# Feed-forward products with the activations standing and 512 weight columns moving

## The reference, cut to what matters

```
x = x + g1 * y                                   # y: the mixer's output
h = rmsnorm(x) * (1 + sc2) + sh2                 # 256 tokens x 1024
x = x + g2 * ((silu(h @ W_gate) * (h @ W_up)) @ W_down)     # width 2816
```

## Time and profile before

| | |
|---|---|
| time, 3 executions | 1597.55, 1596.38, 1596.40 us |
| median | 1596.4 us |
| the profiled execution | span 1595.4 us from its first to its last instruction, 1.0 us under the median |
| PE busy | 1539.4 us, 96% of the span, 12451 matmul records |
| DVE, ACT, POOL busy | 1198.9 us (75%), 785.7 us (49%), 110.9 us (7%) |
| memory traffic | 383.77 MB, 241 GB/s on average |

### The profile page before, as it was taken

One profiled execution on the slowest core, in us unless ns is written; L12 is line 12 of the kernel. 1 busy time (PEld: TensorE's weight loads), 2 busy tenths in 40 slices (PEclk: granted clock), 3 DMA queues, 4 the chain that ended last, 5 costly groups with the idle time before them and its releaser, 6 DMA issues.

```text
span 1595.4 us, 30716 instructions
## 1 busy us (share of the span) xinstructions
PE 1539.4 (96%) x12451; PEld 1470.4 (92%) x12460; DVE 1198.9 (75%) x1724; ACT 785.7 (49%) x1033; POOL 110.9 (7%) x111
## 2 busy tenths in 40 slices
PE   2889999999999999999999999999999999999998
PEld 1868999999999999999899999789999988899998
DVE  6898877778578777865587777968777788676665
ACT  2455433356464333565543335565333577655543
POOL 0150000000000000011000000220000063200000
PEclk9999999999999999999999999999999999999999
DMA  9855987856258878573478785446878655345550
GB/s 389 356 187 213 372 312 298 308 188 236 80 211 327 324 297 325 207 258 132 159 318 323 306 318 206 148 159 253 348 300 312 235 174 183 120 162 183 182 184 26
DMA packets 54907, 383.77 MB, mean 241 GB/s; under 512 B 6420, under 2 KB 6932, under 8 KB 9264
## 3 DMA queue, kind: packets, MB, share of 16 engines
q1 hardware_dynamic: 50976, 363.75, 60.5%
q0 software_dynamic: 3856, 18.97, 3.3%
HBM read 381.62 MB, written 4.22 MB: 242 GB/s over the span
## 4 chain that ended last, share of the span: by engine, by line
PE 85%; DVE 8%; DMA 3%; ACT 1%; issue 1%; POOL 1%; SPq 0%; DVEq 0%; ACTq 0%
PE PS L1929 74%; PE PS L1950 3%; DVE wlo L1359 2%; DVE adar L1384 1%; DMA CST<-cst_in 1%; PE PS L2076 1%; PE PS L2126 1%; DMA adar<-ada 1%; DVE SCR L1546 1%; PE PS L2103 1%; PE PS L2004 1%; ACT whi L930 1%; DMA raw<-ada 1%; PE PS L1976 1%; PE PS L1963 1%
## 5 line engine op out<-in xcount | busy, mean ns | idle before, releaser
L1929 PE MATMUL PS<-hhi,whi 128*128 128x256 f32 x2496 | 714.7, 286 | 2.7 <-DVE wlo L1359 2.6
L1929 PE MATMUL PS<-hlo,whi 128*128 128x256 f32 x2496 | 708.3, 284 | 0.0
L1929 PE MATMUL PS<-hhi,wlo 128*128 128x256 f32 x2496 | 708.1, 284 | 0.0
L1359 DVE TENSOR_TENSOR wlo<-raw,whi 128x2048 fp32r<-128x2048 f32 x229 | 526.3, 2300 | 238.4 <-ACT whi L930 238.1
L930 ACT ACTIVATE whi<-raw 128x2048 fp32r<-128x2048 f32 x234 | 447.0, 1912 | 479.4 <-PE PS L1929 467.1
L1929 PEld LDWEIGHTS PS<-hhi,whi 128*128 128x128 f32 x2496 | 480.9, 193 | 9.8 <-issue 7.7
L1929 PEld LDWEIGHTS PS<-hlo,whi 128*128 128x128 f32 x2496 | 481.3, 193 | 1.3 <-issue 1.2
L1929 PEld LDWEIGHTS PS<-hhi,wlo 128*128 128x128 f32 x2496 | 481.1, 193 | 0.0
L1384 DVE CUSTOM_DVE_ANT_0 adar<-adar,CB 128x1024 f32<-128x1024 f32 x232 | 277.0, 1233 | 9.7 <-DMA adar<-ada 9.7
L1929 PE MATMUL PS<-ahi,whi 128*128 128x256 f32 x968 | 274.5, 284 | 1.1 <-DVE alo L1879 1.1
L1929 PE MATMUL PS<-alo,whi 128*128 128x256 f32 x968 | 273.9, 283 | 0.0
(11 more groups left out here) (240 smaller groups left out, 1319.7 us busy)
## 6 DMA issues: line engine op xcount, KB each, us to landing
raw<-weights SPq DMA_DIRECT2D x234, 1024.0 KB, 6.4
adar<-ada SPq DMA_DIRECT2D x104, 1024.0 KB, 5.8
adar<-ada POOLq DMA_DIRECT2D x12, 1024.0 KB, 5.4
raw<-ada SPq DMA_DIRECT2D x4, 1024.0 KB, 15.2
bias_rows<-bias_of_distance POOLq DMA_DIRECT2D x1, 3072.0 KB, 13.7
adar<-bias_rows POOLq DMA_DIRECT2D x8, 256.0 KB, 3.2
CST<-cst_in SPq DMA_DIRECT2D x1, 1128.0 KB, 22.7
CB<-c_in SPq DMA_DIRECT2D x2, 512.0 KB, 3.8
```

The costliest lines, as they stand in the source:

```text
L1359: v.tensor_tensor(wlo[:, u % CV, :], raw[:, u % RAW, :], whi[:, u % CV, :].bitcast(F32), ALU.subtract).then_inc(lo_done, 1)
L1929: m = pe.matmul(o, w(a), h(b), start=first and k_ == 0, stop=last and k_ == 2, skip_group_check=True)
```

## The change

In the four layers that are not `b2`, a feed-forward step's gate and up columns are packed side by side, 512 columns, and its two units hold the first and the second half of the 1024 input channels (`row_units`). In `row_half` a 128 x 128 block of the activations (128 channels, 128 tokens) stands and 512 weight columns move; the result has tokens on the partitions, one bank for each half of the tokens (`row_banks`). A unit is then 24 matmuls of 512 columns. Silu and the product are done on that layout. `turn_act` brings the product back to channels on partitions with four PE transposes, and `ffn_hi` and `act_lo` read the turned bank in PSUM. `first_rows` takes the place of `project_pair` for step 0.

In all five layers `down` has the activations standing and 512 columns of the down weights moving, for the first ten steps; the sums have tokens on the partitions (`down_rows`). ACT then copies the four banks to SBUF (`down_copies`), PE turns them into the eight half banks with 16 transposes (`turn`), and the eleventh step is added as before (`down_last`). The last two steps are written out behind a loop of four instead of five. The conditions on which engines wait change with the layout, and `act_lo` moves in DVE's queue from behind the third `lo` of a step to behind the first `ada_sum` of the next.

The layout in PSUM:

```diff
+        def row_banks(s_):
+            return PS[:, 2 * (s_ % 2):2 * (s_ % 2) + 2, :]
+        def turned_bank(s_):
+            return bank[2 * (s_ % 2)]
+        def down_rows(t, h):
+            return bank[4 + 2 * h + t]
+        def down_copy(t, h):
+            return SCR[:, (0, 1, 4, 5)[2 * h + t], :]
         def down_bank(c):
-            return bank[4 + c // 2][:, S * (c % 2):S * (c % 2) + S] if c < C - 1 else bank[2][:, 0:S]
+            return bank[(2, 2, 3, 3, 4, 4, 5, 6)[c]][:, S * (c % 2):S * (c % 2) + S]
```

ACT:

```diff
-                        act.wait_ge(pe_unit, (f if s_ == 0 else f + 2 + 3 * (s_ - 1)) + 1 + 6 * add)
+                        act.wait_ge(pe_unit, (f if s_ == 0 else f + 2 + 3 * (s_ - 1)) + 2 + 6 * add)
-                    act.activation(SCR[:, 2, :], src, ACT.Silu).then_inc(sg_done, 1)
+                        act.activation(two(SCR[:, 2, :]), row_banks(s_)[:, :, 0:S], ACT.Silu).then_inc(sg_done, 1)
+                        act.wait_ge(a_turned, STEPS * l + s_ + 1 + 2 * add)
+                        src = turned_bank(s_)[:]
+                    act.activation(ahi[:, s_ % 2, :], src, ACT.Copy).then_inc(ahi_done, 1)
+                def down_copies(h):
+                    for t in range(2):
+                        if (h, t) == (1, 1):
+                            act.wait_ge(pe_unit, f + FFN_UNITS - 1)
+                        else:
+                            act.wait_ge(y_part, 3 * l + 2 * h + t + 1)
+                        act.activation(down_copy(t, h), down_rows(t, h)[:], ACT.Copy).then_inc(y_copied, 1)
...
                         hi(f + 4 + 3 * st, add=i)
+                        if kind != "b2":
+                            ffn_hi(st, add=i)
                         hi(f + 5 + 3 * st, add=i)
                         ffn_gate(1 + st, add=i)
                         hi(f + 6 + 3 * st, add=i)
-                        ffn_hi(1 + st, add=i)
+                        if kind == "b2":
+                            ffn_hi(1 + st, add=i)
+                down_copies(0)
+                if kind != "b2":
+                    ffn_hi(STEPS - 1)
+                down_copies(1)
```

DVE:

```diff
                 ffn_act(0)
                 lo(f + 3)
-                act_lo(0)
+                if kind == "b2":
+                    act_lo(0)
                 if more:
                     ada_sum(a0, 1, a0 % 2)
                 with v.Fori(0, 5) as i:
...
                         lo(f + 4 + 3 * st, add=i)
                         if more:
                             ada_sum(a0 + 1 + st + 2 * i, 0, (a0 + 1 + st) % 2)
+                        if kind != "b2":
+                            act_lo(st, add=i)
                         lo(f + 5 + 3 * st, add=i)
                         if more:
                             ada_sum(a0 + 1 + st + 2 * i, 1, (a0 + 1 + st) % 2)
                         ffn_act(1 + st, add=i)
                         lo(f + 6 + 3 * st, add=i)
-                        act_lo(1 + st, add=i)
+                        if kind == "b2":
+                            act_lo(1 + st, add=i)
```

PE:

```diff
+                def rows_of(u, s_, c, t, parts, first=False):
+                    for x, a in parts:
+                        m = pe.matmul(row_banks(s_)[:, t, :], hs[x][:, c, P * t:P * t + P], ws[a][:, u % CV, 512 * (c % 4):512 * (c % 4) + 512],
+                                      start=first and (x, a) == (0, 0), stop=c == C - 1, skip_group_check=True)
+                    return m
+                def row_half(u, s_, h, add):
+                    unit_ready(u, add)
+                    for t in range(2):
+                        for c in range(4 * h, 4 * h + 4):
+                            m = rows_of(u, s_, c, t, ((0, 0), (0, 1), (1, 0)), c == 0)
+                    m.then_inc(pe_unit, 1)
+                def first_rows(u, m):
+                    warm(4, (4, 5, 6, 7))
+                    unit_ready(u)
...
+                    for c in range(1, C):
+                        pe.wait_ge(norm_lo, C * m + c + 1)
+                        if c == 4:
+                            unit_ready(u + 1)
+                        for t in range(2):
+                            e = rows_of(u + c // 4, 0, c, t, ((0, 0), (0, 1), (1, 0)))
+                        if c % 4 == 3:
+                            e.then_inc(pe_unit, 1)
+                def turn_act(s_, add=0):
+                    pe.wait_ge(a32_done, STEPS * l + s_ + 1 + 2 * add)
+                    for j in range(2):
+                        for t in range(2):
+                            e = pe.transpose(turned_bank(s_)[:, S * j + P * t:S * j + P * t + P], SCR[:, 3, S * t + P * j:S * t + P * j + P], ident)
+                    e.then_inc(a_turned, 1)
...
-                    for c in range(C):
-                        o = down_bank(c)
-                        for t in range(2):
-                            m = split_product(o, lambda a: ws[a][:, u % CV, D * t + P * c:D * t + P * c + P],
-                                              lambda x: acts[x][:, s_ % 2, S * t:S * t + S], False, True)
+                    for h, t in itertools.product(range(2), range(2)):
+                        for j in range(2):
+                            for x, a in ((0, 0), (1, 0), (0, 1)):
+                                m = pe.matmul(down_rows(t, h)[:], acts[x][:, s_ % 2, S * j + P * t:S * j + P * t + P],
+                                              ws[a][:, u % CV, D * j + 512 * h:D * j + 512 * h + 512], start=False, stop=True, skip_group_check=True)
+                        if ready and (h, t) != (1, 1):
+                            m.then_inc(ready, 1)
+                        if last_act and (h, t) == (1, 0):
+                            last_act()
+                def turn(c):
+                    h = c // 4
+                    if c % 4 == 0:
+                        pe.wait_ge(y_copied, 4 * l + 2 * h + 2)
+                    for t in range(2):
+                        pe.matmul(down_bank(c)[:, P * t:P * t + P], down_copy(t, h)[:, P * (c % 4):P * (c % 4) + P], ident,
+                                  start=(t == 0 and c in (0, 2, 4, 6, 7)), stop=True, is_transpose=True, skip_group_check=True)
+                def down_last(u):
+                    for c in range(4):
+                        turn(c)
+                    unit_ready(u)
+                    pe.wait_ge(alo_done, STEPS * l + STEPS)
+                    for c in range(C):
+                        if c == 4:
+                            for k in range(4, C):
+                                turn(k)
+                        for t in range(2):
+                            m = split_product(down_bank(c), lambda a: ws[a][:, u % CV, D * t + P * c:D * t + P * c + P],
+                                              lambda x: acts[x][:, (STEPS - 1) % 2, S * t:S * t + S], False, True)
+                        if c in (1, 3, 5, 6):
+                            m.then_inc(y_done, 1)
+                def ffn_step(st, i, ready=None):
+                    if kind != "b2":
+                        row_half(f + 2 + 3 * st, 1 + st, 0, i)
+                        turn_act(st, i)
+                        row_half(f + 3 + 3 * st, 1 + st, 1, i)
+                        down(f + 4 + 3 * st, st, i, ready, (lambda: turn_act(STEPS - 1)) if ready else None)
+                        return
...
-                project_pair(f, before, 3, high=first_high(plan.split_norm(plan.norm[l] + 1)), cleared=(4, 5, 6, 7, 2), first_low=l + 1)
-                with pe.Fori(0, 5) as i:
+                if kind == "b2":
+                    project_pair(f, before, 4, high=first_high(plan.split_norm(plan.norm[l] + 1)), cleared=(4, 5, 6, 7), first_low=l + 1)
+                else:
+                    first_rows(f, plan.split_norm(plan.norm[l] + 1))
+                with pe.Fori(0, 4) as i:
                     for st in range(2):
+                        ffn_step(st, i)
+                ffn_step(0, 4)
+                ffn_step(1, 4, y_part)
+                down_last(f + FFN_UNITS - 1)
```

More of the change, by code:

```diff
@@ L220, in program @@
         hi_done, lo_done, pe_unit = sem("hi_split"), sem("lo_split"), sem("unit_multiplied")
-        y_done = sem("down_bank_done")
+        a_turned = sem("act_product_turned")
+        y_part, y_copied, y_done = sem("down_rows_summed"), sem("down_rows_copied"), sem("down_bank_done")
         lo_first = sem("second_unit_low_half_first_chunks")
@@ L1868, in ffn_act @@
                     else:
-                        v.wait_ge(pe_unit, (f if s_ == 0 else f + 2 + 3 * (s_ - 1)) + 2 + 6 * add)
-                        val = half_bank(s_, 1)[:]
+                        val = row_banks(s_)[:, :, S:2 * S]
                     v.wait_ge(sg_done, STEPS * l + s_ + 1 + 2 * add)
                     if not (isinstance(add, int) and s_ == 0):
-                        v.wait_ge(alo_done, STEPS * l + s_ + 2 * add)
-                    v.tensor_tensor(SCR[:, 3, :], val, SCR[:, 2, :], ALU.mult).then_inc(a32_done, 1)
```

(32 more changed lines are left out.)

18 lines of the change are left out of this document (13 added, 5 removed).

## The result

The changed kernel takes 1587.6 us (median of four runs, 1586.65 to 1589.26) against 1596.9 for the kernel before on the same chip: a ratio of 0.9941, 95% interval 0.9929 to 0.9952. It is 9.3 us faster. I had forecast 1611 us, 0.9% slower: the sign was wrong. The time of the rival "a fixed cost of each matmul" (1586 us) is the one that came.

What follows compares the result with a forecast made beforehand. PE's matmul stream was taken as the bound. Four layers 3.64 us longer each (14.6) and `b2` -0.2 add 14.4 to the 1595.4 us span, 1609.8; with 1.0 to the median, 1611 us, range 1572 to 1630.

Steps and rivals of the forecast that it cites:

- the sign: Whole kernel: slower with chance 0.66, the same 0.12, faster 0.22; likeliest 1611 us, 0.9% slower.
- a fixed cost of each matmul: Feed-forward matmuls: part of 0.120 us is fixed, so 512 columns cost 0.2275 or 0.2233; 1586 or 1573 us; chance 0.17.
- What bounds the kernel: Feed-forward blocks: PE, busy 96% of the span; only the number of matmuls times their distance sets the time.
- T is 0.235 by the nearest row (same type, same columns), taken as 0.2355: Distance in us between two fp32r matmuls of 512 columns, against 0.240 for two at 256; break-even 0.231.
- the cost grows with the columns: fp32r matmuls: 0.235 us at 512 columns lies between twice 0.1158 and twice 0.120, so little is fixed per matmul.
- next to no load: L694 and L695, standing block of 12 columns: 0.235 us each, taken as evidence against a fixed cost.
- first-step wait: First feed-forward step of four layers: PE waits 0.5 us for `alo`, late behind `ada_sum` in DVE's queue.
- Transposes: Feed-forward block of each non-`b2` layer: 60 added on PE at 0.11 us each, 6.60 us.
- `b2`: Down only: 1.08 us saved, 1.76 of transposes added, 0.9 of them inside an old wait for `alo`: -0.2 us.
- no wait on `a_turned` or `y_copied`, none in later steps: Feed-forward layers: copies have cover, and from the second step `alo` is ready some 4 us ahead; no wait added.
- no time from the clears: `project_pair`'s two clearing matmuls, 0.60 us, ran while the first part of h was made; removing them gains nothing.
- its sum, 47 us faster: Feed-forward matmuls priced by the skill page's 216 ns at 512 columns: the sum would be 47 us faster than before.

Runs made afterwards that it cites:

- Experiments 1 and 6: Runs of 72 matmuls of one shape added behind the changed kernel's last layer; 512 columns with 128 standing settle at 226.8 and 226.7 ns.
- gate and up alone: Changed kernel with down as before, except its last chunk shares the preceding chunk's bank, which is added to x later; 1598.2 us, ratio 1.0007.
- second kernel of runs: Changed kernel with runs of 72 fp32r matmuls added behind the last layer, varying standing columns and partitions; 512 columns with 128 standing settle at 226.7 ns.

## Why the prediction was wrong

- **What bounds the kernel**: right. PE's stream of matmuls set the time before and after, and every experiment moved with its length or with a wait in it.
- **The step that failed is "T is 0.235 by the nearest row (same type, same columns), taken as 0.2355", and with it the reading "the cost grows with the columns".** Long runs in place have 0.2267: for a block of 128 columns a fixed 13.3 ns comes on top of the columns. The two matmuls of the earlier trace rows agree with the change's in type and columns, but their standing block has 12 columns instead of 128, and they are the first two at 512 behind matmuls at 256. Experiments 1 and 6 price both at full clock: 230 to 232 ns for every narrower block tried over 128 partitions, 231 to 237 for most of the first six of a run. Either would do for 0.235; how much each had in the pair stays open, since the pair's own shape has no price at full clock. I had used the narrow block the wrong way round, as a bound with "next to no load". T at 0.2267 in place of 0.2355 is 3312 x 0.0088 = 29.1 us. Put into my sum, it gives 1581.9. The rival of a fixed cost had not only the time but nearly the terms: T of 0.2275, and 1.1 us of first-step wait.
- **Why a 512-column fp32r matmul stays longer with a narrower standing block** was not found; only that it does.
- **Transposes**, 0.11 each and 6.6 us a layer: right, 0.109, and nothing hides them.
- **The first-step wait**: place and cause right (`act_lo` behind `ada_sum`, gone when they change places), size too small: 0.5 against 0.9 listed and 1.2 by the ends. In the first layer PE is ready at 168.50 where I had 169.55, and `alo` at 169.28 where I had 170.05, which makes 0.3 of it; 0.15 more pass from there to PE's start at 169.43, and 0.26 are the longer matmuls behind. 4 x 0.7 = 2.8 us.
- **A term that I did not have**: the longer matmuls behind each turn, 0.03 to 0.05 us in 11 units of a layer, 0.45 us; four layers, 1.8.
- **`b2`**: its wait of the earlier trace rows went as forecast, and 16 transposes and 240 matmuls are what changed. With T at 0.2267 my -0.2 becomes -2.3; measured -1.8. Its down units stand between 256-column ones and take 5.47, not 5.44 (0.3 us in ten).
- **Steps that held**: no wait on `a_turned` or `y_copied`, none in later steps, no time from the clears.

The account of a layer, in order: 768 x 0.0133 = 10.2 us saved, 60 x 0.109 = 6.5 given to transposes, 1.2 to the wait, 0.5 to the longer starts: 2.0, and 1.97 is measured. The whole: 1581.9 + 2.8 + 1.8 + 0.5 = 1587.0 against 1587.6. On the profiled spans it is 1585.8 against 1585.2, so agreement closer than some 0.6 us would be luck.

The Trainium skill, "TensorE: Matmul & The Clock Gate", section "Back-to-back issue gap", has N/2.4 + 2.5 ns, an estimate of 216 ns here. The bfloat16 run agrees (215.8); fp32r has 226.7, so its sum, 47 us faster, was off by more than mine in the other direction: the measurement decides.

One thing is accounted for only in part. Alone, the halves move the time by -7.2 and +0.9 us; together by -9.3. That leaves 3.0 us by the medians, 4.5 by the lengths of the blocks. When only one half is wide, each of its units follows one at 256 columns and starts long: 5.47 for each unit of `down` alone, 5.47 to 5.49 for all units of gate and up alone, in place of 5.44. That is about 0.3 and 0.7 us a layer, against 0.45 in the whole change: some 2 us. The late chunk of gate and up alone is the other part: the `b2` block of that kernel, whose products are as before, takes 196.99 us, 0.43 more than before. If it costs as much in all five layers, an estimate, that is 2.1 us, and 4.3 of the 4.5 us are named; in the other four layers its price was not taken apart.

## What to carry to other kernels

A price is taken from a run of the same shape on both sides, standing block included, long enough to settle; a pair of matmuls at a change of shape prices the change, not the shape. When a sum turns on one price and its break-even (here 0.231) lies between two rows, the spread of the rows is the forecast, and the sign is open. And a step that moves work on the bound engine also moves its deadline: after a gain, look in the producer's queue for what stands ahead of the operand it needs; here one exchange of two entries gave 5.1 us on top of the change's 9.3.

## What the hardware showed that I had not expected

At 512 fp32r columns the first matmuls of a run mostly take 228 to 237 ns and settle at 226.7 after some six to ten, after transposes, after a wait and right behind 256 columns alike; bfloat16 has no such start (215 or 216 from the first).

TensorE's clock fell in a fully busy engine. Windows of the second kernel of runs (stretch, its length, busy time and count of PE, PEld, DVE, ACT and POOL, granted clock, DMA share, GB/s): 512 columns with 32 standing over 128 partitions, then over 32 partitions with 128 and with 12 standing columns, then 256 columns over 128:

```profile
1581.86:1598.50 16.64, 16.64 (x74) 7.90 (x73) 0.08 (x1) 0.00 (x0) 0.00 (x0) 1.00 0.09 30
...
1632.95:1661.50 28.55, 28.55 (x74) 21.36 (x73) 0.00 (x0) 0.00 (x0) 0.00 (x0) 0.55 0.00 1
1662.61:1693.40 30.79, 30.79 (x73) 9.39 (x73) 0.00 (x0) 0.00 (x0) 0.00 (x0) 0.50 0.00 0
1694.47:1704.30 9.83, 9.83 (x74) 9.83 (x73) 0.00 (x0) 0.00 (x0) 0.00 (x0) 0.86 0.01 2
```

PE is busy all the time in each, and yet the granted clock went from 1.00 to 0.50, that is from 2.4 to 1.2 GHz, within the first run over 32 partitions, and came back within the run over 128. That the partitions are the reason is not shown; it is one profile. At the lower level 512 columns take 426.6 ns and 256 take 213.3, exactly the columns at 1.2 GHz: the 13.3 ns that the change saved on do not exist there.
